# Second norm of a decoder layer: the last product and square additions put between the norm's tiles, squares kept in a PSUM bank

## The reference

```
mix = concat([attn_o, conv_o], axis=-1)
h = x + mix @ w_out
hn = rms_norm(h, norm_ffn_g)          # y * rsqrt(mean(y*y) + 1e-6) * g
out = h + (silu(hn @ w_gate) * (hn @ w_up)) @ w_down
```

## Time and profile before

| | |
|---|---|
| median of 3 runs | 1329.93 us (1328.24 to 1329.94) |
| the profiled execution, its own time | 1328.51 us |
| its span | 1326.7 us |
| PE busy in the span | 1302.8 us (98%) |
| DVE, ACT, POOL busy | 477.6, 239.5, 503.1 us |
| granted TensorE clock, mean | 0.997 |

### The profile page before, as it was taken

The page is one execution under the profiler, slowest core; times in us unless marked ns, Lnnn a source line. Parts: engine busy times, 40 slices in busy tenths (PEclk is TensorE's granted clock), DMA queues, the critical chain, the costliest instruction groups (busy, mean ns, idle before and its releaser), DMA issues.

```text
span 1326.7 us, 20794 instructions
## 1 busy us (share of the span) xinstructions
PE 1302.8 (98%) x8488; PEld 1223.6 (92%) x8488; DVE 477.6 (36%) x885; ACT 239.5 (18%) x506; POOL 503.1 (38%) x476
## 2 busy tenths in 40 slices
PE   7999999999999999999999999999999999999996
PEld 7999987989666799899999999999999999999996
DVE  6844222444666333950313131222212130303056
ACT  6001110000777411331000000001010101010114
POOL 3442142222654232415343443434343333344435
PEclk9999999999999999999999999999999999999998
DMA  5534566252121221102011111111111111111103
GB/s 196 207 130 173 180 232 229 73 197 80 49 94 35 97 83 33 64 2 79 33 49 48 48 48 48 48 48 48 48 40 41 48 48 48 48 48 35 62 0 133
DMA packets 38084, 107.84 MB, mean 81 GB/s; under 512 B 4016, under 2 KB 16496, under 8 KB 36208
## 3 DMA queue, kind: packets, MB, share of 16 engines
q1 hardware_dynamic: 38000, 106.60, 23.1%
HBM read 95.73 MB, written 10.85 MB: 80 GB/s over the span
## 4 chain that ended last, share of the span: by engine, by line
PE 93%; DVE 4%; ACT 1%; issue 1%; DMA 0%; DVEq 0%; SPq 0%; ACTq 0%
PE ps L518 20%; PE ps L519 20%; PE ps L520 20%; PE ps L890 6%; PE ps L891 6%; PE ps L892 6%; PE ps L660 3%; PE ps L705 2%; PE ps L684 2%; PE ps L637 1%; PE ps L638 1%; PE ps L639 1%; PE ps L609 1%; PE ps L581 1%; DVE out L1174 1%
## 5 line engine op out<-in xcount | busy, mean ns | idle before, releaser
L518 PE MATMUL ps<-act_hi,w_hi 128*128 128x352 f32 x1608 | 523.1, 325 | 8.4 <-DVE act_lo L1197 8.1
L519 PE MATMUL ps<-act_lo,w_hi 128*128 128x352 f32 x1608 | 516.6, 321 | 0.0
L520 PE MATMUL ps<-act_hi,w_lo 128*128 128x352 f32 x1608 | 516.4, 321 | 0.0
L518 PEld LDWEIGHTS ps<-act_hi,w_hi 128*128 128x128 f32 x1608 | 302.6, 188 | 22.5 <-issue 21.6
L519 PEld LDWEIGHTS ps<-act_lo,w_hi 128*128 128x128 f32 x1608 | 303.2, 189 | 0.2
L520 PEld LDWEIGHTS ps<-act_hi,w_lo 128*128 128x128 f32 x1608 | 302.4, 188 | 0.0
L394 POOL TENSOR_TENSOR gate_cell<-ones 128x1 f32<-128x1 f32 x92 | 18.5, 201 | 675.6 <-PE ps L520 460.8
L398 POOL TENSOR_TENSOR w_lo<-w_stage,w_hi 128x1024 fp32r<-128x1024 f32 x93 | 228.5, 2457 | 7.4
L1515 DVE TENSOR_TENSOR work<-ps,work 128x352 f32<-128x352 f32 x66 | 34.5, 525 | 443.6 <-PE ps L520 443.6
L1525 DVE TENSOR_TENSOR resid<-ps,resid 128x352 f32<-128x352 f32 x240 | 126.1, 525 | 102.6 <-PE ps L892 102.6
L890 PE MATMUL ps<-pair_hi,w_hi 128*128 128x352 f32 x504 | 162.7, 323 | 0.0
(11 more groups left out here) (222 smaller groups left out, 1321.8 us busy)
## 6 DMA issues: line engine op xcount, KB each, us to landing
w_stage<-in_w SPq DMA_DIRECT2D x97, 512.0 KB, 3.5
resid<-in_state_k SPq DMA_DIRECT2D x8, 1792.0 KB, 7.8
v_buf<-in_state_v SPq DMA_DIRECT2D x14, 1024.0 KB, 5.4
resid<-in_xT SPq DMA_DIRECT2D x16, 528.0 KB, 7.3
out_yT<-resid SPq DMA_DIRECT2D x24, 176.0 KB, 1.8
q_d<-out SPq DMA_DIRECT2D x12, 176.0 KB, 4.3
out_kT<-out SPq DMA_DIRECT2D x12, 176.0 KB, 1.9
out_v<-out SPq DMA_DIRECT2D x16, 128.0 KB, 1.7
```

What stands on the lines that cost most here:

```text
L518: pe.matmul(out, hi, rhs_hi, start=first, stop=False)
L519: pe.matmul(out, hi, rhs_lo, start=False, stop=False)
L520: return pe.matmul(out, lo, rhs_hi, start=False, stop=last)
```

## The change

Four things are changed together.

1. Squares of the out-projection go into PSUM: jobs use five banks (`OUT_BANKS = 5`, bank j % 5), and ACT writes every square into the sixth, one at a time. Square j waits until square addition j - 1 has read the bank. The square addition reads PSUM and `ssum`.
2. DVE's square addition j follows product j directly, no longer product j + 1.
3. `norm` becomes `normals`, which writes some of a chunk's tiles. From job 19 on, products and square additions stand between the tiles of chunks 0 and 1, on DVE and ACT alike.
4. The sum of chunk 1 stands behind job 21, no longer behind job 22.

```diff
@@ out_job (PE)
-                if j >= 6:
-                    pe.wait_ge(h_done, j - 5)
+                if j >= OUT_BANKS:
+                    pe.wait_ge(h_done, j - OUT_BANKS + 1)
...
-                    mm = three_pass(ps[:, j % 6, 0:CH], ...
+                    mm = three_pass(ps[:, j % OUT_BANKS, 0:CH], ...
@@ square (ACT)
-                if j >= 6:
-                    act.wait_ge((h_ss, last_ss)[which], j - 5)
-                act.activation(sq6[j % 6], res[:, n, cols(c)], ACT.Square).then_inc(h_sq, 1)
+                if which == 0 and j >= 1:
+                    act.wait_ge(h_ss, j)
...
+                act.activation(sq6[j % 6] if which else ps[:, OUT_BANKS, 0:CH], res[:, n, cols(c)], ACT.Square
+                               ).then_inc(h_sq, 1)
@@ order on ACT
-            for j in range(NC * KT):
-                square(0, j)
-                if j in SUMS_BEHIND:
-                    take_root(1, SUMS_BEHIND.index(j))
-                if j == SUMS_BEHIND[0]:
-                    normal_hi(0)
+            for j in range(SUMS_BEHIND[0] + 1):
+                square(0, j)
+            take_root(1, 0)
+            normal_hi(0, range(0, 2))
+            square(0, 19)
+            normal_hi(0, range(2, 5))
+            square(0, 20)
+            normal_hi(0, range(5, 8))
+            take_root(1, 1)
+            square(0, 21)
...
@@ add_squares (DVE)
-                    dve.tensor_tensor(ssum[:, cols(c)], ssum[:, cols(c)], sq6[j % 6], ALU.add).then_inc(h_ss, 1)
+                    dve.tensor_tensor(ssum[:, cols(c)], ps[:, OUT_BANKS, 0:CH], ssum[:, cols(c)], ALU.add).then_inc(h_ss, 1)
@@ order on DVE
-            for j in range(NC * KT):
-                add_product(0, j)
-                if j >= 1:
-                    add_squares(j - 1)
-                if j in SUMS_BEHIND:
-                    mean_square(1, SUMS_BEHIND.index(j))
-                if j == SUMS_BEHIND[0]:
-                    norm(1, 0)
-            add_squares(NC * KT - 1)
-            norm(1, 1)
+            for j in range(SUMS_BEHIND[0] + 1):
+                add_product(0, j)
+                add_squares(j)
+            mean_square(1, 0)
+            normals(1, 0, range(0, 2))
+            add_product(0, 19)
+            normals(1, 0, range(2, 3))
+            add_squares(19)
+            normals(1, 0, range(3, 5))
+            add_product(0, 20)
+            normals(1, 0, range(5, 6))
+            add_squares(20)
+            normals(1, 0, range(6, 8))
+            add_product(0, 21)
+            mean_square(1, 1)
+            add_squares(21)
+            normals(1, 1, range(0, 1))
+            add_product(0, 22)
+            normals(1, 1, range(1, 2))
+            add_squares(22)
+            normals(1, 1, range(2, 3))
+            add_product(0, 23)
+            normals(1, 1, range(3, 4))
+            add_squares(23)
+            normals(1, 1, range(4, 8))
@@
-SUMS_BEHIND = [18, 22]
+OUT_BANKS = 5
+SUMS_BEHIND = [18, 21]
```

More of the change, by code:

```diff
@@ L1038, in square @@
                 act.wait_ge(h_done, NC * KT * which + j + 1)
-                if j >= 6:
-                    act.wait_ge((h_ss, last_ss)[which], j - 5)
-                act.activation(sq6[j % 6], res[:, n, cols(c)], ACT.Square).then_inc(h_sq, 1)
+                if which == 0 and j >= 1:
+                    act.wait_ge(h_ss, j)
+                if which == 0 and j == 0:
+                    act.wait_ge(act_copied, copied_through(STEPS, 0))
+                    act.wait_ge(dve_copied, copied_through(STEPS - 1, 1))
+                if which == 1 and j >= 6:
+                    act.wait_ge(last_ss, j - 5)
+                act.activation(sq6[j % 6] if which else ps[:, OUT_BANKS, 0:CH], res[:, n, cols(c)], ACT.Square
+                               ).then_inc(h_sq, 1)
             def first_silu():
@@ L1049, in _ @@
             first_silus = first_silu()
-            for j in range(NC * KT):
+            for j in range(SUMS_BEHIND[0] + 1):
                 square(0, j)
-                if j in SUMS_BEHIND:
-                    take_root(1, SUMS_BEHIND.index(j))
-                if j == SUMS_BEHIND[0]:
-                    normal_hi(0)
+            take_root(1, 0)
[6 more added lines that the diff above has]
+            square(0, 21)
+            normal_hi(1, range(0, 1))
+            square(0, 22)
+            normal_hi(1, range(1, 3))
+            square(0, 23)
+            normal_hi(1, range(3, 4))
             next(first_silus)
-            normal_hi(1, range(0, 2))
+            normal_hi(1, range(4, 8))
             next(first_silus)
-            normal_hi(1, range(2, 8))
             take_root(1, 2)
[L1061 to L1065, removed]
+            normal_hi(2, range(0, 8))
             def gates(it, g, first=False):
@@ L1175, in normal, with normals @@
                                          ALU.mult, ALU.mult).then_inc(y_done, 1)
-            def norm(which, c):
+            def normals(which, c, ks):
                 def low(i):
@@ L1183, in low @@
                                       ALU.subtract).then_inc(lo_done, 1)
-                for k in range(KT):
+                for k in ks:
                     i = KT * c + k
@@ L1191, in norm @@
                         low(i - 1)
-                low(KT * c + KT - 1)
+                    if k == KT - 1:
+                        low(i)
             def raw_low(k):
@@ L1482, in add_product @@
                     dve.wait_ge(x2_in[n], 16)
-                bank = j % 6 if which == 0 else last_bank(j)
+                bank = j % OUT_BANKS if which == 0 else last_bank(j)
                 dve.tensor_tensor(res[:, n, cols(c)], ps[:, bank, 0:CH], res[:, n, cols(c)],
@@ L1490, in add_squares @@
                 if n == 0:
[L1491 removed]
+                    dve.tensor_copy(ssum[:, cols(c)], ps[:, OUT_BANKS, 0:CH]).then_inc(h_ss, 1)
                 else:
                     dve.wait_ge(h_ss, OUT_ORDER.index((n - 1, c)) + 1)
[L1494 to L1496 removed]
+                    dve.tensor_tensor(ssum[:, cols(c)], ps[:, OUT_BANKS, 0:CH], ssum[:, cols(c)], ALU.add).then_inc(h_ss, 1)
+            for j in range(SUMS_BEHIND[0] + 1):
                 add_product(0, j)
[L1498 to L1505 removed]
+                add_squares(j)
[21 more added lines that the diff above has]
+            normals(1, 1, range(4, 8))
             mean_square(1, 2)
[L1507 removed]
+            normals(1, 2, range(0, 8))
             def hidden_of(it, g, first=False):
```

2 lines of the change are left out of this document (1 added, 1 removed).

## The result

The changed kernel takes 1333.99 us (median of 7 runs, 1333.59 to 1335.01) against 1329.79 us before (7 runs, 1328.24 to 1330.03). The ratio is 1.0035, with a 95% interval from 1.0025 to 1.0044: slower by some 4.2 us. The profiled execution took 1334.11 us, its span is 1332.3 us and its mean granted clock 0.994.

What follows compares the result with a forecast made beforehand. PE, 93% of the chain, was taken to bound the kernel, so only its waits count. Terms -1.0, -2.27 plus 0.2, -0.57 plus 6.6, -0.2 and clock 2.3 gave +5.1 us: 1334.5 us, range 1328.5 to 1337.5.

Steps and rivals of the forecast that it cites:

- the sum: All changes in PE's waits, +2.8 us, plus 2.3 us for the clock: +5.1 us in total.
- Parts 1 and 2, the first sum: Chunk 0's sum on PE follows job 18 without its 1.05 us wait, squares in PSUM costing nothing: gain 1.0 us.
- Part 3, the second sum: Chunk 1's sum behind job 21 starts at 540.15 us, waiting 0.2 us instead of 2.27: gain 2.0 us.
- Where the order turns, the third sum: Last sum, behind FFN job (0, 0), needs addition 23, ending at 559.05 us: PE waits 6.6 us instead of 0.57.
- the order of turns: On DVE, a scaled or low tile waits out POOL's running instruction, then POOL's next goes in.
- The scaled tile contends: On DVE, scaled tiles contend with POOL too: 1.95 us for two instead of 1.08.
- The clock: Behind the third sum's wait, 17 matmul steps at 0.293 us instead of 0.159 lose 2.3 us; bounds 0 to 2.6.
- a choice between two bases: Total time: profiled execution plus 5.1 gives 1333.6 us, the median before gives 1335.0; 1334.5 was taken between.
- DVE keeps up: Rival at the third sum: contention costs DVE under 3 us, net -3.3 us, 1325 to 1327 us; chance 0.17.

Runs made afterwards that it cites:

- thin_splits: The changed kernel with POOL splitting only 16 of 1024 columns of the first three FFN weight tiles, the fourth behind chunk 1's low tiles: 1324.47 us, ratio 0.9968.
- early23: The changed kernel with the steps of jobs 22 and 23 ahead of chunk 1's reciprocal and tiles, on DVE and ACT: 1324.02 us, ratio 0.9963.
- rstd_psum: The changed kernel with the second norm's mean, root and reciprocal in PSUM, so the scaled tile has one SBUF input: 1331.38 us, ratio 1.0019.
- kept_warm: The changed kernel with 42 extra, unused matmuls on PE between job (0, 0) and the third sum: 1331.83 us, ratio 1.0024.
- sbuf_squares: The changed kernel with the squares back in six SBUF slots, five banks kept for the jobs: 1333.22 us, ratio 1.0035.
- late_mean: The changed kernel reordered: chunk 0's tiles spread over jobs 19 to 21, additions 21 to 23 ahead of chunk 1's reciprocal: 1323.20 us, again 1323.13 us.
- direct_psum: The kernel before with only squares in the PSUM bank and each square addition directly behind its product: 1329.74 us, ratio 1.0006.

## Why the prediction was right

The direction, the mechanism and the size came out: +4.87 us in the stage where the sum said +5.1, and 1333.99 us where 1334.5 was named. Point by point, with the 0.76 us of the later start taken off:

**Parts 1 and 2, the first sum.** Predicted: no idle, gain 1.0. Measured: no idle, gain 1.32. Three rows of the kernel before show the missing 0.3:

```profile
527.18 0.32 PE L520 MATMUL ps<-act_hi,w_lo 128*128 128x352 f32 x1
...
528.98 0.59 PE L518 MATMUL ps<-pair_hi,w_hi 128*128 128x352 f32 x1
529.41 0.33 PE L519 MATMUL ps<-pair_lo,w_hi 128*128 128x352 f32 x1
```

From the last matmul ahead of the sum to the second behind it took 2.23 us with 1.05 us idle, so 1.18 without it; in the kernel after it took 0.91 (527.94 to 528.85). A sum that has waited costs 0.27 us more than its idle time says. The rows place all of it. 0.16 is a matter of counting: the idle time is counted from the end of the row at 527.18, 0.32 us on, while without a wait the next matmul starts 0.16 us behind the start of the last. 0.11 is the sum's own step, 0.43 us to the next matmul (528.55 to 528.98) where the unwaited sum has 0.32 (528.10 to 528.42). The prediction read that addition 17 could run 3.4 us earlier; it ran 3.2 us earlier. The addition from PSUM took 0.52 to 0.53 as assumed, and the square into PSUM 0.47 us in ACT's timeline, against the 0.50 that I took:

```profile
521.23 0.47 ACT L1046 ACTIVATE ps<-resid 128x352 f32<-128x352 f32 x1 [3.34 <-DVE resid L1495]
```

**Part 3, the second sum.** Predicted: addition 20 at 539.6 to 540.1, the sum at 540.15, wait 0.2. Measured: it ended at 540.05, the sum started at 540.11, wait 0.57. The walk on DVE was exact; the wait was larger because PE, with its first sum unwaited, was free at 539.54, 0.4 us before I had it. What PE gains ahead of a wait it hands over to that wait.

**Where the order turns, the third sum.** Predicted 6.6, measured 7.59. The step that failed by 1 us is the order of turns at chunk 1's first tile. I let scaled tile 0 end before POOL's third subtraction, with tile 1 blocked by it. In the trace the subtraction starts at 550.92 and tile 0 at 550.95, 0.03 us too late, and takes 2.75 us. So the three blocked instructions were scaled 0, scaled 1 (0.92 us, by the copy) and low 0, one place further forward than scaled 1, low 0 and scaled 2; seven instructions instead of five were left behind the fourth subtraction, which is 0.9 us. The number of blocked instructions was right, and so was the end of POOL's fourth subtraction (556.4 predicted and measured). `thin_splits` and `early23` show both conditions of this step: contention and the order.

**The scaled tile contends.** Put on the single row of 1.95 us for two. The 2.75 us above and `rstd_psum` bear it out. The Trainium skill, SBUF — State Buffer, section "Who interferes with whom", says that a VectorE instruction with two SBUF inputs contends with a GpSimd instruction that reads SBUF. The scaled tile has two SBUF tiles as inputs, so it falls under that rule, and the trace agrees (2.75 us for 0.58). The prediction looked only at the list of operations further down in that section, which names `tensor_tensor` and not this form, and took the omission for a rule that scaled tiles don't block; the section doesn't say so. The forecast doesn't hang on it.

**The clock.** Predicted 2.3, measured 1.66 by the rows and some 1.5 by `kept_warm`. The traces of the two kernels differ by 1.64 us. That it falls was right, the size was not: I had carried over the 17 slow steps of the program's start, and here there were the sum's two passes and 7 steps. The prediction let the whole slow stretch fall on matmuls; but the granted clock was at 0.50 from near 557.5 us on, and 3.3 us of the low level passed while PE was waiting anyway. The bounds of 0 to 2.6 held here.

**The sum.** -1.32 - 1.70 + 7.02 + 1.66 - 0.8 stands against -1.0 - 2.07 + 6.03 + 2.3 - 0.2. A wait 1 us longer was made up by a clock 0.6 cheaper and by gains ahead and behind that were 0.5 us larger; the hit within 0.5 us is partly that. The late start of the profiled execution isn't part of the change, and the medians give 4.2 us, 3.3 to 5.9 by the interval. The named 1334.5 also rests on a choice between two bases; +5.1 on the median before of 1329.79 would have been 1334.9, 0.9 us too much.

**The rivals.** "DVE keeps up" was named as what contention under 3 us would give, 1325 to 1327. `thin_splits` made the end of that case, no contention, and came out below it, at 1324.47 beside a kernel before of 1328.28: -3.8 us, where -3.3 had been reckoned.

## What to carry to other kernels

Interleaving on an engine moves work forward and work back: walk the order down to the last thing that the bounding engine waits for, with each instruction's duration beside the neighbour that contends with it, and put everything that PE needs next ahead of what it needs later. An instruction with two SBUF inputs beside a stream of GpSimd work took up to five times its price here (2.70 us for 0.53), so the one that is waited for is the one to give a PSUM input. In `sbuf_squares`, where tiles stood blocked ahead of the addition anyway, the bank was worth nothing; in `late_mean` it was worth 3.0 us. And ask of each gain what else starts sooner because of it: in `direct_psum` the earlier PE brought POOL's split onto DVE's tiles, which, with the waits for ACT, gave the gain back.

## What the runs showed of the hardware

- **A waited sum costs more than its idle row.** 0.27 us over the idle time, at full clock (1.18 against 0.91 us between the same two matmuls). 0.16 of it is how the profile counts idle time, 0.11 the sum's longer step to the next matmul (0.43 against 0.32). Why that step is longer, the rows don't show.
- **The clock's fall.** Behind 2.27 us of idle in the middle of the program the matmul lasted 0.86 us at full clock, behind 3.99 us (`direct_psum`) 1.54 us at the slow level, which I had not expected of a wait that short. The number of slow matmuls behind a wait doesn't follow its length: 6 at 0.293 us behind 7.59 us, 15 behind 4.76 us (`rstd_psum`). The windows of the granted clock show why. In the changed kernel it is at 0.50 from 557.5 to 564.0 us and the sum starts at 560.76, so 3.3 us of the low level lie in the wait. In `rstd_psum` it is at 0.50 to 0.52 from 556.5 to 563.0 us and the sum starts at 557.17, so nearly all of a low stretch as long falls on matmuls.
- **One turn each.** A blocked DVE instruction ends 0.38 us behind POOL's, and POOL's next one is stretched in turn: its copy took 1.29 to 1.42 us beside DVE's blocked instructions in the changed kernel, and 1.04 at 549.80 us beside the reciprocal. The reciprocal, with one SBUF input, stayed at 2.34 to 2.35 us in every kernel that has it in SBUF.
- **The start varies.** Executions of the same program up to there placed the first sum at 526.9 to 528.10 us. In a comparison of two profiles, count from a common instruction.
